# Constant products in the waits of the norms, and modulation columns spread through a tile

## What is computed

```
mod = jax.nn.silu(c) @ w_ada[l] + b_ada[l]
sh1, sc1, g1, sh2, sc2, g2 = jnp.split(mod[:, None, :], 6, axis=-1)
h = x * (1.0 + sc1) + sh1
y = token_mixer(h, ...)
x = layer_norm(DEEPNORM_ALPHA * x + g1 * y, ln1_g[l], ln1_b[l])
h = x * (1.0 + sc2) + sh2
y = conv_ffn(h, ...)
x = layer_norm(DEEPNORM_ALPHA * x + g2 * y, ln2_g[l], ln2_b[l])
```

## Time and profile before

| | |
|---|---|
| median of three runs | 2498.26 us |
| the profiled execution | 2498.26 us, span 2496.4 us |
| PE busy | 2405.9 us, 96% of the span |
| DVE, ACT, POOL busy | 48%, 40%, 40% |
| mean clock granted to TensorE | 0.986 of full speed |

### The profile page before, as it was taken

The page is one execution under the profiler, slowest core; times in us unless marked ns, Lnnn a source line. Parts: engine busy times, 40 slices in busy tenths (PEclk is TensorE's granted clock), DMA queues, the critical chain, the costliest instruction groups (busy, mean ns, idle before and its releaser), DMA issues.

```text
span 2496.4 us, 32249 instructions
## 1 busy us (share of the span) xinstructions
PE 2405.9 (96%) x11364; PEld 1889.9 (76%) x11364; DVE 1205.1 (48%) x2594; ACT 1006.0 (40%) x1677; POOL 997.1 (40%) x812
## 2 busy tenths in 40 slices
PE   7999999999999999999999999999999989999998
PEld 4778767778888876776677888887788867777756
DVE  7565665654344357567466343313340172244584
ACT  6444344344343244543433344423242353333463
POOL 3452222444444443413144444444444433444342
PEclk9999999999999999999999999999999999999999
DMA  8531134312226243212341222223222210222210
GB/s 334 216 112 67 45 108 148 123 68 101 99 75 238 93 187 135 80 44 88 128 152 68 97 88 101 82 99 108 84 85 84 101 73 34 84 85 85 85 43 35
DMA packets 52133, 259.68 MB, mean 104 GB/s; under 512 B 6385, under 2 KB 16369, under 8 KB 26417
## 3 DMA queue, kind: packets, MB, share of 16 engines
q1 hardware_dynamic: 50864, 249.76, 28.3%
q0 software_dynamic: 1152, 8.39, 0.8%
HBM read 249.61 MB, written 7.34 MB: 103 GB/s over the span
## 4 chain that ended last, share of the span: by engine, by line
PE 78%; issue 11%; POOL 4%; DVE 4%; ACT 2%; DMA 1%; DVEq 0%; POOLq 0%; SPq 0%; ACTq 0%
PE bank L718 21%; PE bank L720 21%; PE bank L719 21%; POOL w_lo L583 4%; PE bank L937 3%; PE bank L831 2%; PE bank L942 1%; PE bank L1197 1%; PE bank L855 1%; PE bank L1114 1%; PE bank L979 1%; PE bank L844 1%; PE bank L1186 1%; PE bank L1333 1%; DMA ada_early<-w_ada 0%
## 5 line engine op out<-in xcount | busy, mean ns | idle before, releaser
L583 POOL TENSOR_TENSOR w_lo<-w_raw,w_hi 128x512 fp32r<-128x512 f32 (+1 forms) x692 | 880.9, 1305 | 1304.5 <-ACT w_hi L1385 872.8
L718 PE MATMUL bank<-h_hi,w_hi 128*128 128x512 f32 x1616 | 658.8, 408 | 12.8 <-POOL w_lo L583 8.8
L720 PE MATMUL bank<-h_hi,w_lo 128*128 128x512 f32 x1616 | 632.5, 391 | 0.0
L719 PE MATMUL bank<-h_lo,w_hi 128*128 128x512 f32 x1616 | 631.0, 390 | 0.0
L718 PEld LDWEIGHTS bank<-h_hi,w_hi 128*128 128x128 f32 x1616 | 304.6, 188 | 92.7 <-issue 26.8
L720 PEld LDWEIGHTS bank<-h_hi,w_lo 128*128 128x128 f32 x1616 | 303.9, 188 | 65.5
L719 PEld LDWEIGHTS bank<-h_lo,w_hi 128*128 128x128 f32 x1616 | 304.6, 188 | 64.4 <-issue 7.0
L1385 ACT ACTIVATE w_hi<-w_raw 128x2048 fp32r<-128x2048 f32 (+1 forms) x114 | 201.4, 1766 | 291.0 <-PE bank L720 239.4
L2221 DVE SCALAR_TENSOR_TENSOR cv<-bank,par,cv 128x511 f32<-128x511 f32 (+1 forms) x176 | 131.6, 749 | 215.4 <-ACT cv L1627 201.0
L1627 ACT ACTIVATE cv<-bank,par 128x512 f32<-128x512 f32 x88 | 68.4, 779 | 235.4 <-PE bank L720 231.8
L1461 ACT ACTIVATE L<-L,nmax 128x128 f32<-128x128 f32 (+3 forms) x128 | 72.0, 563 | 191.7 <-DVE nmax L1952 191.3
(11 more groups left out here) (392 smaller groups left out, 3923.0 us busy)
## 6 DMA issues: line engine op xcount, KB each, us to landing
w_raw<-w_stream SPq DMA_DIRECT2D x150, 1024.0 KB, 4.8
w_raw<-w_down SPq DMA_DIRECT2D x32, 704.0 KB, 4.0
ada_mid<-w_ada SPq DMA_DIRECT2D x20, 1024.0 KB, 5.0
ada_last<-w_ada SPq DMA_DIRECT2D x12, 1024.0 KB, 4.8
ada_early<-w_ada POOLq DMA_DIRECT2D x8, 1024.0 KB, 20.8
ada_late<-w_ada SPq DMA_DIRECT2D x8, 1024.0 KB, 6.7
bias_in<-bias_scratch SPq DMA_DIRECT2D x16, 256.0 KB, 3.0
bias_in<-bias_scratch SPq DMA_DIRECT2D x16, 192.0 KB, 2.7
```

Source lines behind the costliest of these rows:

```text
L583: ins = nc.gpsimd.tensor_tensor(w_lo[r][:, part], w_raw[r][:, part], w_hi[r][:, part].bitcast(fp32), ALU.subtract)
L718: nc.tensor.matmul(out, w[0][:, cols], xh, start=first, stop=False)
L719: nc.tensor.matmul(out, w[0][:, cols], xl, start=False, stop=False)
L720: return nc.tensor.matmul(out, w[1][:, cols], xh, start=False, stop=last)
```

## The change

Two things are added and one is spread out. `keep_warm(bank, count)` issues `count` products of a matrix of ones with the identity (128x128, float32) into a bank that nothing reads at that time. Twelve of them stand in each of the four layer norm tails: three before PE waits for tile 7 in `x`, four before it waits for the inverse deviation, five behind the spreading products. Fourteen stand in the second block's norm: four before and ten behind `token_rows(2)`. `ada_group` no longer issues its columns: it returns a function that `tile` calls after each chunk, and which issues two of them. They so stand inside tile 6 of the output projection and inside the first half of tile 7 of layer 0's down projection.

```diff
-            def tile(out, w, at, xh, xl, ks, k0=0, first=True, last=True):
+            def tile(out, w, at, xh, xl, ks, k0=0, first=True, last=True, between=None):
                 for k in range(ks):
                     ins = mm3(out, w, slice(at + k * P, at + (k + 1) * P), xh[:, k0 + k, :], xl[:, k0 + k, :],
                               first and k == 0, last and k == ks - 1)
+                    if between:
+                        between(k)
                 return ins
+
+            def keep_warm(bank, count):
+                for _ in range(count):
+                    nc.tensor.matmul(banks[bank][:, 0:P], ones, ident, start=True, stop=True)
...
             def ada_group(first, halves, late, bank):
-                pe.wait_ge(ada_used, 2 * (first + halves))
                 part = first % 12 - 4 if first % 12 else 0
-                for j in range(4 * halves):
-                    ins = nc.tensor.matmul(banks[bank][:, j:j + 1], ...
-                ins.then_inc(ada_sum, 1)
+                def columns(k):
+                    if k == 0:
+                        pe.wait_ge(ada_used, 2 * (first + halves))
+                    for j in range(2 * k, min(2 * k + 2, 4 * halves)):
+                        ins = nc.tensor.matmul(banks[bank][:, j:j + 1], ...
+                        if j == 4 * halves - 1:
+                            ins.then_inc(ada_sum, 1)
+                return columns
...
                 elif f == 7:
+                    pe.wait_ge(tile_evac, tdone(l, t + 6))
+                    keep_warm(0, 3)
                     pe.wait_ge(tile_evac, tdone(l, t + 7))
                     nc.tensor.matmul(banks[5][:, :], mean_w, x[:, 7, :], start=False, stop=True).then_inc(rest_done, 1)
                     by_token(2, x[:, 7, :]).then_inc(tok_done, 1)
                     pe.wait_ge(sq_ready, KD * (k + 1))
                     by_token(7, ln_sq[1]).then_inc(sq_used, 1)
+                    keep_warm(0, 4)
                     pe.wait_ge(inv_ready, k + 1)
...
                     ins.then_inc(rep_done, 1)
+                    keep_warm(0, 5)
...
             mean_squares(7, sqp[1])
+            keep_warm(4, 4)
             token_rows(2)
+            keep_warm(4, 10)
             swap_loop(2, SLOT2_K2, TILE2_K2, 4, k2, 16, mean_w, 1, 5)
```

More of the change, by code:

```diff
@@ L752, in ada_group @@
             def ada_group(first, halves, late, bank):
-                pe.wait_ge(ada_used, 2 * (first + halves))
                 part = first % 12 - 4 if first % 12 else 0
-                for j in range(4 * halves):
-                    ins = nc.tensor.matmul(banks[bank][:, j:j + 1],
-                                           ada_acc[late][:, part + j // 4, (j % 4) * P:(j % 4 + 1) * P],
-                                           ones[:, 0:1], start=True, stop=True)
-                ins.then_inc(ada_sum, 1)
+                def columns(k):
+                    if k == 0:
+                        pe.wait_ge(ada_used, 2 * (first + halves))
+                    for j in range(2 * k, min(2 * k + 2, 4 * halves)):
+                        ins = nc.tensor.matmul(banks[bank][:, j:j + 1],
+                                               ada_acc[late][:, part + j // 4, (j % 4) * P:(j % 4 + 1) * P],
+                                               ones[:, 0:1], start=True, stop=True)
+                        if j == 4 * halves - 1:
+                            ins.then_inc(ada_sum, 1)
+                return columns
             pe.sem_inc(tile_done, TILE_PRE)
@@ L1071, in _ @@
                     if f < 7:
-                        ins = tile(banks[f % 2][:, :], split(l, SLOT_OUT + f // 2), (f % 2) * D, m_hi, m_lo, KD)
+                        if f == 6:
+                            pe.wait_ge(tile_evac, tdone(l, TILE_BRB + 6))
+                        ins = tile(banks[f % 2][:, :], split(l, SLOT_OUT + f // 2), (f % 2) * D, m_hi, m_lo, KD,
+                                   between=ada_group(12 * l + 9, 3, 0, 6) if f == 6 else None)
                     else:
@@ L1078, in _ @@
                     norm_stats(l, 0, f)
-                    if f == 5:
-                        pe.wait_ge(tile_evac, tdone(l, TILE_BRB + 6))
-                        ada_group(12 * l + 9, 3, 0, 6)
                 first_slot(l, SLOT_UP, TILE_UP, h_hi, h_lo, h_hid, KD * hidx(l, 1), h_ready, KD * hidx(l, 1))
@@ L1095, in down @@
                             norm_early(l, 1)
-                        ins = tile(banks[f % 2][:, :], split(l, SLOT_DOWN + s), 0, u_hi, u_lo, 11, 11 * s, s == 0, s == 1)
+                        if l == 0 and f == 7 and s == 0:
+                            pe.wait_ge(x_turned, KD)
+                        ins = tile(banks[f % 2][:, :], split(l, SLOT_DOWN + s), 0, u_hi, u_lo, 11, 11 * s, s == 0, s == 1,
+                                   between=ada_group(12, 4, 1, 6) if l == 0 and f == 7 and s == 0 else None)
                         ins.then_inc(tile_done if s else half_done, 1)
@@ L1101, in _ @@
                     norm_stats(l, 1, f)
-                    if l == 0 and f == 6:
-                        pe.wait_ge(x_turned, KD)
-                        ada_group(12, 4, 1, 6)
             def swap_loop(l, m, t, slots, dst, swaps, matrix, which, tables):
```

## The result

The change is slower. Nine runs of it have a median of 2506.70 us (2498.31 to 2508.99), nine of the kernel before 2499.74 us (2497.07 to 2503.19). The ratio is 1.0028, with a 95% interval of 1.0019 to 1.0037. That is 7 us more, where 11 us less were forecast. The profiled execution took 2506.70 us and has a span of 2504.9 us, 8.5 us more than the one before. One of the nine runs of the change, the 2498.31 us one, lost nothing against the kernel before; no trace of it was kept, so it stays open why.

What follows compares the result with a forecast made beforehand. PE, busy for 96% of the span, was taken as the bound, so time is won only where it waits or runs slowly. 2.9 + 6.6 + 1.7 + 0 = 11.2 us off 2498.26 gave 2487.1 us, range 2483.5 to 2493.5.

Steps and rivals of the forecast that it cites:

- Step 1: Columns in the output and down projections: spreading them in twos avoids a clock fall in each layer; 2.9 us won.
- Step 2: First slots behind the four norms: they run at full clock, 1.3 and 2.0 us shorter per layer; 6.6 us won.
- Step 3: Spreading products in the four norms: at most 3.3 us can come back at full clock; half taken, 1.7 us.
- Step 4: Cost of the constant products in the norm tails: they hide in PE's waits; zero taken for all twelve.
- Step 5: Second block's norm: four and ten products fit their waits at full clock; between +0.4 and -1.4 us, zero taken.
- Waiting alone lowers the clock: Rival: the columns were not the cause, so their spreading is worth -0.35 us, the rest holds; 2490.3 us, 10%.
- The slower rival: Constant products outrun their cover in the waits if the clock isn't held; 6.5 us lost, 2501.9 us, 3%.

Runs made afterwards that it cites:

- e3: The change plus nine constant products into bank 6 ahead of the wait for bank 0 in front of tile 6: 2492.91 us, ratio 0.9975.
- e4: The change, with DVE at tile 4 of both projections taking the mean from chunk 4 first, adding tile 4, then the other seven chunks: 2488.91 us.
- e8: The kernel before with only DVE's order turned at tile 4, as in e4: 2498.37 us, ratio 0.9995.
- e5: The change, with the output projections' twelve columns in fours behind the first three chunks of tile 6: 2502.26 us, ratio 1.0011.
- e6: The change, with the output projections' twelve columns in threes behind the first four chunks of tile 7, none in tile 6: 2495.82 us.
- e9: The change, with the output projections' columns one behind each chunk of tile 6 and the first four of tile 7: 2496.10 us, ratio 0.9986.
- e1: The kernel before with the constant products alone, columns left in one piece: 2494.36 us, ratio 0.9981.
- e2: The change without any constant products, only the columns spread: 2513.37 us, ratio 1.0060.
- e7: e4 with six instead of four constant products ahead of the spreading, and fifteen more at the end of the retention: 2486.50 us, ratio 0.9944.

## Why the prediction was wrong

The forecast was 2487.1 us and faster; it is 2506.7 us and slower. The step that failed is the first.

- **Step 1, the columns: 2.9 us won were forecast, 14.1 us were lost.** The sentence "between twos of columns three dense matmuls (0.68 us) keep PE working" is true at full clock (e3, e4), and the price of 0.02 us a pair was right. What was left out is that the columns were cover. I asked who waits for the columns, and not what PE would do in their place. The rows needed were in DVE's timeline: tile 4 added at 483.96, tile 6 free to begin at 482.66. Of the 7.0 us in each layer, 2.15 are this wait, now bare; 0.1 is the interleaving; and 4.8 are half clock (6.4 us lost in place of 1.62). e3, e4 and e8 show the wait as the trigger, e5, e6 and e9 the columns as what holds the clock down.
- **Step 2, the first slots: right, 6.0 us for a forecast of 6.6.** The slots are 1.2, 1.9, 1.1 and 1.9 us shorter (forecast 1.3 and 2.0 a layer) in the change, and the same in e1. e2, without the products, has none of it beyond 0.25 us.
- **Step 3, the spreading: 0.3 us instead of 1.7 in this profile.** In three of four norms a fall still comes right there, as in the row 514.57:516.10 at 0.63, and is over by the slot. It is a matter of where the fall lands. With the same four products ahead of it, the four norms together win 1.8 us in e1, nothing in e3 and 1.8 to 2.1 us in e4, e5, e6 and e9; e7, with six products, has 2.7 us of the 3.3. So the size of the term came out in most profiles, and that of the change is one of the two poor ones.
- **Step 4, the cover of the constant products: right for the change.** The way from tile 7 to the spreading is unchanged to 0.02 us in it. The overrun that the prediction feared at half clock does occur elsewhere: behind layer 0's down projection in e9 a fall came upon the four products, their eight records took 2.04 us, and the spreading came 0.3 us later. In e5 and e6 one norm each is 0.1 to 0.2 us later.
- **Step 5, the second block: about right.** 0.9 us less in place of 0, of which 0.8 lie ahead of the norm, at the end of the retention, where a fall was shorter; the slot won 0.1.
- **The rivals.** "Waiting alone lowers the clock" had -0.35 us for step 1: it had the wait as a cause, but I didn't see that the change makes one. The Trainium skill (TensorE: Matmul & The Clock Gate, oscillation) has idle time between bursts as the cause of a fall. e6 agrees, with 2.04 us of wait and slow matmuls 0.5 us later. The falls behind columns in one piece, at PE busy throughout, remain outside it, and the wait of 2.96 us without a fall speaks against taking it as certain. The slower rival (constant products outrun their cover) was the wrong mechanism: in the change they fit, at 0.22 us each. The right sign on the slower side needed a wait uncovered, which none of the rivals named.

What stays open: why a piece of twelve columns lowers the clock at one place each time, and one of sixteen in the down projection did so in e1 and not in the kernel before or in e8. Open is also why the wait ahead of tile 6 brought a fall each time and the longer one at 71 us didn't. So is the scatter of falls at places that no edit touched, which makes some 2 us of any single profile.

## What to carry to other kernels

Before work is moved away from a place, look at what the engine would wait for there: read on the engine that frees the next buffer when it does so, and compare with the time at which the moved work began, not ended. Small one-column products between dense chunks cost little at full clock, but thin them out so that a clock that has fallen can come back under them, and don't put them right behind a bare wait. Constant products in waits that can't be removed cost little where they fit (nothing in the change; 0.3 us in e9 and 0.9 us in e7, each time where a fall came upon them), and their gain is not the wait but the first dense work behind it.

## What the hardware showed that was not expected

- A fall holds itself up. At half clock a chunk with two columns takes 2.14 us instead of 1.14, and in this rhythm the clock stayed down for over 13 us; with one column for each chunk it was down for 3.4 us.
- A wait of 2.0 us between dense tiles was followed by a fall in the change, e2, e5, e6 and e9, in both layers. It isn't so everywhere: behind 2.96 us at 71 us of the kernel before the clock stayed at 1.00.
- Nine constant products in that wait (e3) were enough to prevent it, though they are ones times the identity, 128 columns wide.
- The mean clock over the span doesn't rank these two kernels: 0.987 with 7 us more, 0.986 before. What a fall costs depends on what it lies over: some 3.4 us of dense matmuls lost 1.62 us to it, and one that lay on the spreading products delayed DVE and the slot by 0.4 to 0.9 us (the falls that e7 is rid of).
